# Layer 1's shared expert moved behind its seventh group, eighteen weight homes, and half-piece first reuses in layer 2

## The reference, cut to what matters

```python
# block 1: 64 experts (1024 -> 256 -> 1024), 8 for each token, and one shared expert for every token
s = sigmoid(hf @ w_router);  idx = top_k(s + b_router, 8);  wts = s[idx] / sum(s[idx]) * 2.5
for e in range(64):
    y[rows of e] += wts * ((silu(hf @ we_gate[e]) * (hf @ we_up[e])) @ we_down[e])
y += (silu(hf @ ws_gate) * (hf @ ws_up)) @ ws_down        # the shared expert
# block 2: attention, pooling and gates, then 32 experts (1024 -> 512 -> 1024), 2 for each token
for e in range(32):
    y = y + combine[:, e:e+1] * ((silu(hf @ w_g[e]) * (hf @ w_u[e])) @ w_d[e])
```

## Time and profile before

| | value |
|---|---|
| median of 3 executions | 1389.51 us (1387.2 to 1389.67) |
| the profiled execution | 1387.14 us |
| its span, first to last instruction | 1385.2 us |
| mean granted TensorE clock | 0.924 of full speed |
| PE busy | 1156.9 us (84%) |
| DVE / ACT / POOL busy | 347.8 / 187.6 / 85.3 us |
| moved by DMA | 509.40 MB, mean 368 GB/s |

### The profile page before, as it was taken

How to read it: one execution, slowest core, us unless ns; L and a number is a source line. 1 busy time by engine, 2 the same in 40 slices (tenths; PEclk the granted TensorE clock), 3 DMA queues, 4 the chain that set the end, 5 groups by cost and what they waited for, 6 DMA issues and landing times.

```text
span 1385.2 us, 21371 instructions
## 1 busy us (share of the span) xinstructions
PE 1156.9 (84%) x9078; PEld 634.1 (46%) x9078; DVE 347.8 (25%) x926; ACT 187.6 (14%) x385; POOL 85.3 (6%) x117
## 2 busy tenths in 40 slices
PE   5999999999999999999989999997466474665556
PEld 3664454655555555555547588753122121222212
DVE  1598576411111111111112143352010000100002
ACT  1210123211111111111122023031000000000000
POOL 2499000000000000000000000000000000000000
PEclk9999999999999999999999999999778786777888
DMA  9879983899999999999996423949999999999996
GB/s 388 344 308 422 407 371 139 318 417 421 418 420 419 419 420 420 420 420 420 420 402 219 187 110 144 397 200 382 428 427 427 428 428 427 429 427 426 428 425 236
DMA packets 54420, 509.40 MB, mean 368 GB/s; under 512 B 6630, under 2 KB 8846, under 8 KB 14130
## 3 DMA queue, kind: packets, MB, share of 16 engines
q1 hardware_dynamic: 50985, 502.03, 87.1%
q10 hardware_dynamic: 3338, 5.98, 1.4%
HBM read 506.92 MB, written 2.64 MB: 368 GB/s over the span
## 4 chain that ended last, share of the span: by engine, by line
PE 51%; DMA 27%; SPq 17%; issue 3%; DVE 2%; ACT 1%; DVEq 0%; ACTq 0%
SPq L663 12%; PE PS L1833 6%; PE PS L1659 6%; DMA W<-in_w_expert_down 5%; PE PS L1177 5%; DMA W<-in_w_expert_up 4%; DMA W<-in_w_expert_gate 4%; PE PS L1742 4%; SPq L661 3%; PE PS L1671 3%; PE PS L1123 3%; PE PS L1518 3%; DMA scr<-in_w_expert_gate 2%; PE PS L1198 2%; DMA hx<-in_w_expert_up 2%
## 5 line engine op out<-in xcount | busy, mean ns | idle before, releaser
L1833 PE MATMUL PS<-W,scr 128*32 128x512 f32 x640 | 142.8, 714 | 85.0 <-DMA W<-in_w_expert_gate 20.6
L1659 PE MATMUL PS<-W,scr 128*32 128x256 f32 (+1 forms) x1648 | 170.0, 381 | 2.6 <-DMA W<-in_we_up 1.7
L1833 PE MATMUL PS<-scr 128*32 128x512 f32 x288 | 108.9, 725 | 60.4 <-DMA W<-in_w_expert_gate 32.9
L2365 DVE TENSOR_TENSOR scr<-scr,PS 128x256 f32<-128x256 f32 (+1 forms) x33 | 23.4, 709 | 506.0 <-PE PS L1833 262.9
L1659 PEld LDWEIGHTS PS<-W,scr 128*32 128x32 f32 (+1 forms) x1648 | 92.8, 115 | 52.4 <-issue 12.4
L1518 PE MATMUL PS<-scr 128*128 128x512 f32 x248 | 114.7, 605 | 0.0
L1833 PEld LDWEIGHTS PS<-W,scr 128*32 128x32 f32 x640 | 34.5, 129 | 146.6 <-issue 100.9
L1492 PE MATMUL PS<-scr 128*128 128x128 bf16 x1536 | 93.5, 222 | 0.0
L943 ACT COPY scr<-PS 128x512 f32<-128x512 f32 x66 | 38.6, 587 | 403.0 <-PE PS L1492 400.3
L1659 PE MATMUL PS<-scr 128*32 128x256 f32 (+1 forms) x816 | 90.3, 380 | 2.1 <-DMA W<-in_we_up 2.1
L1492 PEld LDWEIGHTS PS<-scr 128*128 128x128 bf16 x1536 | 91.0, 100 | 1.0 <-issue 0.6
(11 more groups left out here) (433 smaller groups left out, 1446.0 us busy)
## 6 DMA issues: line engine op xcount, KB each, us to landing
W<-in_we_gate SPq DMA_DIRECT2D x45, 1024.0 KB, 25.0
W<-in_we_down SPq DMA_DIRECT2D x41, 1024.0 KB, 25.1
W<-in_w_ada SPq DMA_DIRECT2D x10, 4096.0 KB, 14.7
W<-in_w_expert_gate SPq DMA_DIRECT2D x20, 2048.0 KB, 29.9
W<-in_w_expert_up SPq DMA_DIRECT2D x20, 2048.0 KB, 29.4
W<-in_we_up SPq DMA_DIRECT2D x34, 1024.0 KB, 24.9
W<-in_w_expert_down SPq DMA_DIRECT2D x16, 2048.0 KB, 32.2
scr<-in_we_up SPq DMA_DIRECT2D x20, 1024.0 KB, 25.0
```

The source lines that it names most:

```text
L1659: m = mm(PS[4 + kind][at:at + size, 0:F1], hTe[:, k, at:at + size], piece_view((g, kind, j))[:, k, :], start=(k == 0), stop=(k == KD - 1))
L1833: m = mm(PS[4 + kind][j * CAP2:(j + 1) * CAP2, :], hTe[:, k, j * CAP2:(j + 1) * CAP2], piece_view2((g, kind, j))[:, k, :], start=(k == 0), ...
```

## The change

Layer 1: `features` is no home any more, so there are eighteen. The shared expert's three pieces leave `KNOWN_AHEAD` (twelve are left) and stand in `READ1` and `LOADS1` at the place where they are read: gate and up behind group 6, down behind group 7. Its gate and up matmuls now run in one block behind group 6's down matmuls, 64 of 256 columns in place of 32 of 512, and write banks 6 and 7, for which PE first waits on `x_Y`. Its transposes stand in group 7, its down matmuls behind group 7. ACT's silu and DVE's product go behind their group 6. In the sort, PE's `loads` is cut into `counts` (which waits for the mask alone) and `order_of`, nothing of the shared expert stands between the steps, and `order` gets its matmul and copy ahead of the rest; on DVE `sort_places` comes before the four `left_of_h`, and the copy of `order` after the first of them.

Layer 2: the pieces 10 to 13, which are the first to take over homes (those of group 0's gate pieces), are loaded in halves: the first halves wait for one half of the gate matmuls (`e2_gateup` 1), the second halves for both. A sixth late counter (`HALF_RING`) takes the first halves.

```diff
@@ -86,26 +86,26 @@
 SLOTS, SLOT_WORDS = 12, 2048
-PLACES1 = [5, 6, 8, 9, 10, "scratch0", 0, 1, 2, 3, 4, 11, "scratch1", "scratch2", 7, "scratch3", "gates", "rows", "features"]
+PLACES1 = [1, 2, 4, 5, 7, 8, 9, 10, 11, 0, 3, 6, "scratch0", "scratch1", "scratch2", "scratch3", "gates", "rows"]
...
 PIECES1 = [(-1, kind, 0) for kind in range(3)] + [(g, kind, j) for g, group in enumerate(GROUPS1) for kind in range(3) for j in range(len(group))]
-SHARED_BEHIND = 3
-KNOWN_AHEAD = [p for p in PIECES1 if p[0] < 0 or GROUPS1[p[0]][p[2]][0] < STATIC1]
-KNOWN_AHEAD = [p for p in KNOWN_AHEAD if p != (-1, 2, 0)] + [(-1, 2, 0)]
-LOADS1 = KNOWN_AHEAD + [p for p in PIECES1 if p not in KNOWN_AHEAD]
-FILLED1 = sorted(range(len(KNOWN_AHEAD)), key=lambda i: PLACES1[i] if PLACES1[i] in range(12) else 12 + i)
-READ1 = [p for p in PIECES1 if p != (-1, 2, 0)]
-READ1.insert(READ1.index((SHARED_BEHIND + 1, 0, 0)), (-1, 2, 0))
+SHARED_BEHIND = 6
+KNOWN_AHEAD = [p for p in PIECES1 if p[0] >= 0 and GROUPS1[p[0]][p[2]][0] < STATIC1]
+READ1 = [p for p in PIECES1 if p[0] >= 0]
+at = READ1.index((SHARED_BEHIND + 1, 0, 0))
+READ1[at:at] = [(-1, 0, 0), (-1, 1, 0)]
+READ1.insert(READ1.index((SHARED_BEHIND + 2, 0, 0)), (-1, 2, 0))
+LOADS1 = KNOWN_AHEAD + [p for p in READ1 if p not in KNOWN_AHEAD]
+FILLED1 = sorted(range(len(KNOWN_AHEAD)), key=lambda i: PLACES1[i])
...
     RING[piece] = PLACES1[i] if i < len(PLACES1) else RING[READ1[i - len(PLACES1)]]
-SETS1 = [(-1, kind) for kind in range(3)] + [(g, kind) for g in range(NG1) for kind in range(3)]
+SETS1 = list(dict.fromkeys(piece[0:2] for piece in READ1))
...
 LATE1 = (len(SETS1) % 12, (len(SETS1) + 2) % 12)
-assert SETS1.index((SHARED_BEHIND, 2)) < len(SETS1) - 24
@@ -115,7 +115,9 @@
         (F2 // P - 1, 1): 2 * SETS2 + LAST_SET % SETS2 - 1}
-assert len({*LATE1, *LATE.values()}) == 5
+HALVES2 = (len(PLACES2), len(PLACES2) + G2)
+HALF_RING = 2 * SETS2 + 1
+assert len({*LATE1, *LATE.values(), HALF_RING}) == 6
@@ -523,9 +525,7 @@
             return w_o[:, k, :] if k < AHEAD else w_o_ahead[:, k - AHEAD, :]
-        sh_first = RING[-1, 0, 0]
-        assert RING[-1, 1, 0] == sh_first + 1
-        sh_gu = W[:, sh_first * SLOT_WORDS:(sh_first + 2) * SLOT_WORDS].rearrange("p (c k n) -> p c k n", c=2, k=KD)
+        sh_gu = [piece_view((-1, kind, 0)) for kind in range(2)]
@@ -725,6 +725,10 @@
                 sp.dma_start(dst[:, rows_of, columns], src[:, rows_of, columns]).then_inc(S[f"ring{i // G2 % SETS2 if ring is None else ring}"], 16)
+            def halves_at(i):
+                return (F2 // P if PIECES2[i][1] == 2 else KD) // 2
@@ -741,7 +745,13 @@
             fill((9,))
-            for i in range(len(PLACES2), G2 * LAST_SET):
+            sp.wait_ge(S["e2_gateup"], 1)
+            for i in range(*HALVES2):
+                load2(i, slice(0, halves_at(i)), ring=HALF_RING)
+            for i in range(*HALVES2):
+                consumed2(PIECES2[i - len(PLACES2)])
+                load2(i, slice(halves_at(i), None))
+            for i in range(HALVES2[1], G2 * LAST_SET):
@@ -956,9 +966,17 @@
                             a.copy(Y[:, h * 512:(h + 1) * 512], PS[6 + h][:]).then_inc(S["x_Y"], 1)
+                def shared_silu():
+                    for b in range(NB):
+                        act.wait_ge(S["sh_gateup"], b + 1)
+                        step(a.activation(sg_sh[:, b, :], PS[6 + b][:, 0:F1], ACT.Silu), S["sh_sg"], wait=False)
...
                     body(g, last=g == NG - 1)
+                    if L == 1 and g == SHARED_BEHIND:
+                        shared_silu()
@@ -1006,9 +1024,6 @@
                     split_h(1, part, n)
-            for b in range(NB):
-                act.wait_ge(S["sh_gateup"], b + 1)
-                step(a.activation(sg_sh[:, b, :], PS[6 + b][:, 0:F1], ACT.Silu), S["sh_sg"], wait=False)
@@ -1433,7 +1448,7 @@
                             last.then_inc(S["backT"], 1)
-            def loads():
+            def counts():
@@ -1442,16 +1457,21 @@
                 last.then_inc(S["sort_mm"], 1)
+            def order_of():
+                pe.wait_ge(S["sort_made"], 2)
...
                 last.then_inc(S["sort_mm"], 1)
+                pe.wait_ge(S["sort_made"], 3)
+                mm(PS[4][:, 448:512], Sw[0:E1, 1, 0, :], perm[0:E1, :], start=True, stop=True).then_inc(S["sort_mm"], 1)
...
             def sort():
-                pe.wait_ge(S["sort_made"], 2)
-                mm(PS[4][:, 448:512], Sw[0:E1, 1, 0, :], perm[0:E1, :], start=True, stop=True)
+                pe.wait_ge(S["sort_made"], 4)
@@ -1540,11 +1560,13 @@
                         over_list(L)
+                    if L == 1 and g == SHARED_BEHIND + 1:
+                        shared_turned()
...
                     m.then_inc(S["x_turned"], 1)
-                    if first and L == 1:
+                    if L == 1 and g == SHARED_BEHIND + 1:
@@ -1558,13 +1580,16 @@
                     if L == 1 and g == SHARED_BEHIND:
+                        pe.wait_ge(S["x_Y"], 2 * g + 2)
+                        for b in range(NB):
+                            shared_gateup(b)
+                    if L == 1 and g == SHARED_BEHIND + 1:
...
                     gather(0)
-                    shared_turned()
@@ -1614,12 +1639,15 @@
                 pe.wait_ge(S[f"ring{SETS1.index((g, kind)) % 12}"], 16 * LANDED1[g, kind])
-            def shared_gateup(b, half):
-                for k in range(4 * half, 4 * half + 4):
-                    last = mm(PS[6 + b][:].rearrange("t (c n) -> t c n", c=2), hT[:, k, b * P:(b + 1) * P], sh_gu[:, :, k, :],
-                              start=(k == 0), stop=(k == KD - 1))
-                if half:
-                    last.then_inc(S["sh_gateup"], 1)
+            def shared_gateup(b):
+                for kind in range(2):
+                    if not b:
+                        landed(-1, kind)
+                    for k in range(KD):
+                        last = mm(PS[6 + b][:, kind * F1:(kind + 1) * F1], hT[:, k, b * P:(b + 1) * P], sh_gu[kind][:, k, :],
+                                  start=(k == 0), stop=(k == KD - 1))
+                last.then_inc(S["sh_gateup"], 1)
@@ -1631,7 +1659,7 @@
             def shared_down():
-                landed(SHARED_BEHIND, 2)
+                landed(-1, 2)
@@ -1639,16 +1667,11 @@
                 last.then_inc(S["sh_down"], 1)
-            for kind in range(2):
-                landed(-1, kind)
...
             pe.wait_ge(S["gates_made"], 2)
-            shared_gateup(0, 0)
-            loads()
-            shared_gateup(0, 1)
+            counts()
+            order_of()
...
             sort()
-            shared_gateup(1, 0)
...
             ranks(1, E1)
-            shared_gateup(1, 1)
@@ -1824,6 +1847,9 @@
                 pe.wait_ge(S[f"ring{part}"], 16 * RING_USES[part] + 16 * G2 * (turn + 1))
+                halves = sum(piece[0:2] <= (g, kind) for piece in PIECES2[slice(*HALVES2)])
+                if halves and (g, kind) <= PIECES2[HALVES2[1] - 1][0:2]:
+                    pe.wait_ge(S[f"ring{HALF_RING}"], 16 * RING_USES[HALF_RING] + 16 * halves)
@@ -2276,14 +2302,17 @@
                 step(v.tensor_reduce(place, above, AX_X, ALU.add))
-                step(v.tensor_tensor(perm, iota[:, 0:E1], place.to_broadcast([P, E1]), ALU.is_equal))
-                dve.wait_ge(S["sort_mm"], 2)
-                step(v.tensor_copy(turned[0:E1, :, :], PS[5][0:E1, :].rearrange("p (n t) -> p n t", n=4)), S["sort_made"])
-            def sorted_routes():
+                step(v.tensor_tensor(perm, iota[:, 0:E1], place.to_broadcast([P, E1]), ALU.is_equal), S["sort_made"])
+            def order_copied():
...
                 step(v.tensor_copy(order, PS[4][:, 448:512]), S["order_known"])
+                step(v.tensor_copy(turned[0:E1, :, :], PS[5][0:E1, :].rearrange("p (n t) -> p n t", n=4)), S["sort_made"])
+            def sorted_routes():
+                dve.wait_ge(S["sort_mm"], 4)
@@ -2300,6 +2329,9 @@
                     step(v.tensor_tensor(a_sh[:, b, :], sg_sh[:, b, :], PS[6 + b][:, F1:2 * F1], ALU.mult), S["sh_act"])
+            def shared_features():
@@ -2364,6 +2396,8 @@
                                     PS[5][:, 0:F].rearrange("s (p c) -> s p c", p=P), ALU.mult).then_inc(S["x_act"], 1)
+                    if L == 1 and g == SHARED_BEHIND + 1:
+                        shared_features()
@@ -2387,10 +2421,11 @@
                 if L == 1:
-                    shared_act()
...
                     body(g, g % 2, last=g == NG - 1)
+                    if L == 1 and g == SHARED_BEHIND:
+                        shared_act()
@@ -2437,16 +2472,18 @@
                 step(v.match_replace(mask[:, b, :], max8[:, b, :], tmpr[:, b, :], NEG))
-            step(v.tensor_tensor(mask, mask, tmpr, ALU.not_equal))
+            step(v.tensor_tensor(mask, mask, tmpr, ALU.not_equal), S["sort_made"])
...
                      S["sort_made"] if b else None)
-            for n in range(4):
+            sort_places()
+            left_of_h(1, 0)
```

(13 more changed lines are left out.)

## The result

The changed kernel takes 1392.19 us (median of 21 executions, 1389.38 to 1395.53) against 1389.51 (1386.74 to 1392.13), a ratio of 1.0024 with a 95% interval of 1.0016 to 1.0032. By the ratio that is 3.3 us slower, by the two medians 2.7 us. The interval lies above 1, so the kernel is slower; whether by more than the 2.8 us that I called no change stays undecided, since they lie between the two figures. I had forecast 1391.0 us. The profiled execution took 1389.38 us, its span is 1387.6 us; with the same execution of before at 1387.14 I had forecast 1388.6 for it.

The account below looks back on a forecast made before the run. In layer 1 PE and the weights' stream were taken to finish together, in layer 2 the stream bounds. Layer 1's +4.5 and the halves' -3.0 gave +1.5 us, median 1391.0; range 1386.0 to 1395.0, own range 1389.3 to 1392.7.

Parts of the forecast that it names:

- The sort, and when `order` is known: Sort ahead of layer 1's experts: `order` is known 5.7 us earlier, with the first issue at 251.3.
- Part 2: Layer 1's stream: restarts 5.7 us earlier with three pieces (7.5 us) more to bring, so 1.8 us later in all.
- Part 4: Layer 1's experts: PE gains 16.0 us of work; PE's side ends +4.6 us, the stream's +4.3, taken as +4.5.
- the fourth rival: Layer 1: PE's work is hidden after all, +1.8 - 3.0 = -1.2 us or less, 1388 to 1386; chance 0.07.
- The start of group 0: Layer 1's first group: gathering 5.5 us earlier, less 2.3 for the clock's fall, so 3.2 us earlier, at 264.1.
- The stream of layer 1: Layer 1's weights: three pieces (7.5 us) more behind a group 0 that starts 3.2 us earlier, 4.3 us late in all.
- Eighteen homes do not bind: Layer 1's homes: when PE comes to group 8, 79 pieces are out, 76 of them the groups', and 66 read.
- Layer 2's halves: Group 0's gate matmuls in layer 2: half pieces go out before the queue runs dry, -3.0 us, bounds 0 and -3.5.
- The rival that they bring nothing: Layer 2's halves gain nothing, layer 1's loss stands alone: +4.5 us, 1394.0; chance 0.15.
- The signs of being wrong: Waits for weights stay although PE is later; group 0 starts before 262 or after 266; DMA rate dips at the halves.
- The third, a second stretch at half clock: Group 0 of layer 1: the clock rises only after the gathering, another 2.3 us, 1393.3; chance 0.15.
- That the clock would stay up: Rival at group 0's start: the clock doesn't fall, -2.3 on the sum, 1388.7, or 1386.4 with the lowest execution; chance 0.18.

Follow-up runs that it names:

- The third run: The kernel before with `order` known early and the shared gate and up matmuls kept between the steps of the sort: 1388.76 us, ratio 0.9998.
- The eleventh run: The changed kernel with seven unread matmuls in the idle places of the sort: 1392.11 us, ratio 1.0024.
- the twelfth: The kernel before with eighteen homes, `features` being no home: 1391.72 us, ratio 1.0022.
- Runs 5 to 9: Kernel before plus 8 or 16 us unread PE work: 0.9995, 1.0045; changed kernel with an eighth of shared work, 2.25 MB less load, both: 1.0029, 0.9994, 0.9986.
- the eighth run: The changed kernel with 2.25 MB less to load for the shared expert, all TensorE work kept: 1388.37 us, ratio 0.9994.
- the first run: The kernel before with layer 2's half pieces alone: 1386.63 us, ratio 0.9979.
- runs 4 and 11: The changed kernel with five unread matmuls in the idle places of the sort (1391.75 us, ratio 1.0016), and with seven (1392.11 us, ratio 1.0024).

## Why the prediction was right, point by point

The forecast was +1.5 us; measured are +2.7 by the medians and +3.3 by the ratio. The direction and both parts were right in sign. The time lies 1.2 us over the forecast, inside its own range. I had given "slower by over 2.8 us" 0.31, and the ratio's 3.3 is just there.

- **The sort, and when `order` is known.** Right to 0.1 us (5.7 us earlier).
- **What the early `order` is worth.** Part 2 was wrong: it took the 5.7 us off the stream's 7.5 and left 1.8. The third run, in which `order` comes as early and the shared matmuls stay, has 0.9998. Part 4 had the stream right by another count (group 0's start), so the sum was not touched. But the fourth rival used the 1.8.
- **The start of group 0: the mis-sized term.** The fall of the clock came as forecast, but I took 2.3 us from the nearest row. It lasted some 13 us, and group 0 started only 2.0 us earlier (267.33 - 232.53 = 34.8, against 263.83 - 231.02 = 32.8), not 3.2. The eleventh run puts the fall's price at 3.2 us; that is 0.9 of the 1.2 missing. That the gates stand at 263.83, so near the forecast 264.1, is luck: 1.5 us of it come from ahead of the first issue.
- **The stream of layer 1.** I had 7.5 us for three pieces of lead less group 0's earlier start, 4.3 in all. Measured 5.3; with the measured 2.0 the same sum gives 5.5. It also holds for the eleventh run (7.5 - 5.2 = 2.3, measured 2.1). That the lead is worth so much rests on the homes: the third run shows that issuing earlier is worth nothing while the next home isn't free, and the twelfth that a home less costs about a piece.
- **PE's work.** 16.0 us was right (16.4 measured). But I called PE's side and the stream's side equal, +4.6 and +4.3. Runs 5 to 9 part them: PE alone would have ended 2.1 us late by the ratios and 3.4 by the profile (the eighth run), the stream 5.3 late, and the stream decides. The same comes from the slack: 16.4 - 2.0 - 11 = 3.4. I had counted the waits that PE could save at 8.2 us; it is some 11. A fall of the clock at 528 to 536 us (0.79 in the kernel before), which I had overlooked, is 1.7 of the difference; the rest is not accounted for. So the +4.5 was near for one of its two reasons only.
- **"Eighteen homes do not bind"** was wrong as a sentence: I had looked at group 8 alone. At group 0 they bind (the issue at 268.26, and the 321 GB/s behind it). The stream's sum holds without a term for it.
- **Layer 2's halves.** Right: -2.9 us by the first run against -3.0. The rival that they bring nothing fell, and with it the estimate from the Trainium skill's 341 GB/s ("DMA: Bandwidth & Descriptors", "Bandwidth"); that section's rule asks for transfers of at least 1 MiB, which the halves still are.
- **The signs of being wrong.** Two of the three that I had named came in small: 1.9 us of waits for weights stay although PE is later, which is the sign that the stream decides, and the DMA rate dips to 205 GB/s for 2 us where the halves go. I had set no size for either, and both were too weak to move the time out of the range.
- **The rivals.** The third, a second stretch at half clock, had its condition met (the clock rose at about 263, when the gathering was all but over), but its price was 0.9 us, not 2.3. The fourth had its second condition met too, the stream alone decides; its -1.2 was wrong, because it took the stream's shift at Part 2's 1.8 us in place of 5.3. That the clock would stay up fell.
- **What is open.** The idle time of PE in front of the closing matmuls in runs 4 and 11. And the 1.8 us from layer 1's end to layer 2's gates in the two single executions may be chance: the execution after has more time at low clock there (0.70 from 736 to 744 us, where before has 1.00); it was not tested.

Of the kernels that compute the whole output, the kernel before with layer 2's halves alone has the lowest ratio, 0.9979, and is the only one whose interval lies under 1.

## What to carry to other kernels

When a stream of weights and an engine end together, moving work off the start of the stage gains only if the stream is fed there: price each piece of lead, and each home, at the time of one transfer (2.5 us here), and look which home is free next before crediting an earlier issue. Work that fills an engine during another engine's chain costs little, and here it also kept TensorE's clock up for what came right behind (the gathering took 2.84 us, without it 5.25). A test that adds unread work tells slack from bound better than adding up waits: here 9.2 us cost nothing and 16.9 us cost 6.3, where the waits gave 8.2 of slack.

## What the runs showed of the hardware that I had not expected

PE was never idle for more than 2.6 us in one piece between the routing and group 0, yet the granted clock fell to its lower level, 1.2 of 2.4 GHz, among the small matmuls of the sort and stayed there up to about 263 us, through a dense gathering of 5.25 us (granted 0.50 over 250 to 256); with the idle places filled in the eleventh run it stayed at 2.4 GHz (granted 1.00 over 243 to 262). Halves of 1 MB in a full queue moved at 419 GB/s, the rate of 2 MB pieces at that place. And with five and seven matmuls added to PE's program, 2.6 and 4.0 us of idle time stood at a place 460 us further on in the one execution profiled of each; the cause was not tried.
